# Hybrid decoder trunk on one core: value product with stationary values, division ahead of the transposes, norm over channels, output units split sooner

## The reference, cut to what matters

```python
h = rmsnorm(x, norm1_g[l]) * (1.0 + scale1) + shift1
u = h @ w_in[l]
u_b, u_c, u_h, u_q, u_k, u_v = jnp.split(u, split_at, axis=-1)
y_conv = short_conv_mixer(u_b, u_c, u_h, conv_w[l])
q = rope(rmsnorm(heads(u_q), q_norm_g[l]), positions)
k = rope(rmsnorm(heads(u_k), k_norm_g[l]), positions)
y_att = moba_attention(q, k, heads(u_v)).transpose(0, 2, 1, 3).reshape(B, S, aw)
y_mix = jnp.concatenate(
    [rmsnorm(y_conv, conv_out_g[l]), rmsnorm(y_att, attn_out_g[l])], axis=-1)
x = x + gate1 * (y_mix @ w_out[l])
```

## Time and profile before

| | |
|---|---|
| median of 3 runs | 548.28 us (546.69 to 549.7) |
| the profiled execution | 548.4 us, its span 546.5 us |
| TensorE matmul busy | 527.7 us, 97% |
| VectorE busy | 297.9 us, 55% |
| ScalarE busy | 219.2 us, 40% |
| DMA moved | 189.76 MB, mean 347 GB/s |
| chain that ended last | PE 84%, DVE 6%, DMA 4%, ACT 3% |

### The profile page before, as it was taken

The page is one execution under the profiler, slowest core; times in us unless marked ns, Lnnn a source line. Parts: engine busy times, 40 slices in busy tenths (PEclk is TensorE's granted clock), DMA queues, the critical chain, the costliest instruction groups (busy, mean ns, idle before and its releaser), DMA issues.

```text
span 546.5 us, 8062 instructions
## 1 busy us (share of the span) xinstructions
PE 527.7 (97%) x3226; PEld 344.4 (63%) x3226; DVE 297.9 (55%) x498; ACT 219.2 (40%) x386; POOL 18.6 (3%) x76
## 2 busy tenths in 40 slices
PE   6799999998999999999999999999998999999995
PEld 6568997776756444444346889987875544444433
DVE  3638988777783022122258769799976112222233
ACT  2518546552246322222148344864255331222221
POOL 3104100000000000000000000000000000000000
PEclk9899999999899999999999999999999899999998
DMA  8999998199999999999999996413679999999962
GB/s 297 386 387 365 397 404 334 79 396 421 417 410 411 364 416 411 413 413 417 416 399 390 388 410 243 170 63 134 252 274 412 413 367 416 413 413 413 413 273 80
DMA packets 52222, 189.76 MB, mean 347 GB/s; under 512 B 4723, under 2 KB 4819, under 8 KB 44885
## 3 DMA queue, kind: packets, MB, share of 16 engines
q1 hardware_dynamic: 50784, 185.62, 86.4%
q0 software_dynamic: 1072, 2.45, 1.3%
q10 hardware_dynamic: 324, 1.13, 0.6%
HBM read 188.12 MB, written 1.06 MB: 346 GB/s over the span
## 4 chain that ended last, share of the span: by engine, by line
PE 84%; DVE 6%; DMA 4%; ACT 3%; SPq 1%; issue 1%; DVEq 0%; ACTq 0%
PE ps L1857 20%; PE ps L1599 13%; PE ps L1883 10%; PE ps L1606 10%; PE ps L1733 5%; PE ps L1837 5%; PE ps L1899 5%; PE ps L1457 4%; DMA raw<-in_w_ada_dram 2%; DMA raw<-in_w_out_dram 2%; PE ps L1580 1%; PE ps L1652 1%; DVE act_lo L1245 1%; PE ps L1660 1%; PE ps L1448 1%; SPq L381 1%
## 5 line engine op out<-in xcount | busy, mean ns | idle before, releaser
L895 DVE TENSOR_TENSOR wlo<-raw,whi 128x1024 fp32r<-128x1024 f32 x64 | 75.8, 1219 | 16.5 <-ACT whi L581 16.3
L581 ACT ACTIVATE whi<-raw 128x1024 fp32r<-128x1024 f32 x64 | 65.3, 1059 | 35.5 <-DMA raw<-in_w_out_dram 15.5
L1857 PE MATMUL ps<-raw,qkT 128*64 128x512 f32 x256 | 58.8, 611 | 0.0
L1883 PE MATMUL ps<-raw,work 128*64 128x512 f32 x256 | 57.7, 593 | 0.0
L1857 PE MATMUL ps<-raw,cbc 128*64 128x512 f32 x256 | 57.0, 595 | 0.4 <-ACT work L840 0.4
L1599 PE MATMUL ps<-act_hi,whi 128*128 128x256 f32 x192 | 55.1, 287 | 0.1
L1599 PE MATMUL ps<-act_hi,wlo 128*128 128x256 f32 x192 | 54.3, 283 | 0.0
L1599 PE MATMUL ps<-act_lo,whi 128*128 128x256 f32 x192 | 54.3, 283 | 0.0
L1370 DVE SCALAR_TENSOR_TENSOR work<-ps,cw,work 128x256 f32<-128x256 f32 x16 | 10.8, 676 | 78.5 <-ACT work L834 78.5
L1362 DVE TENSOR_TENSOR wlo<-v_sb,whi 128x512 fp32r<-128x512 f32 x32 | 21.0, 688 | 51.6 <-ACT whi L824 51.2
L1883 PEld LDWEIGHTS ps<-raw,work 128*64 128x64 f32 x256 | 18.2, 137 | 36.1 <-issue 35.4
(11 more groups left out here) (275 smaller groups left out, 902.7 us busy)
## 6 DMA issues: line engine op xcount, KB each, us to landing
raw<-in_w_ada_dram SPq DMA_DIRECT2D x36, 1024.0 KB, 14.0
raw<-in_w_gate_dram SPq DMA_DIRECT2D x64, 512.0 KB, 9.6
raw<-in_w_up_dram SPq DMA_DIRECT2D x64, 512.0 KB, 11.0
raw<-in_w_down_dram SPq DMA_DIRECT2D x32, 1024.0 KB, 11.2
raw<-in_w_in_dram SPq DMA_DIRECT2D x23, 1024.0 KB, 14.5
raw<-in_w_ada_dram SPq DMA_DIRECT2D x16, 512.0 KB, 11.7
raw<-in_w_out_dram SPq DMA_DIRECT2D x8, 1024.0 KB, 10.4
cbc<-in_w_ada_dram SPq DMA_DIRECT2D x2, 1024.0 KB, 10.2
```

The source lines that it names most:

```text
L581: act.activation(whi[:, slot(n), :], raw[:, r, (i % 2) * 1024:(i % 2 + 1) * 1024], ACT.Copy).then_inc(hi_done, 1)
L895: dve.tensor_tensor(wlo[:, slot(n), :], raw[:, ring_slot[("w", l, i // 2)], (i % 2) * 1024:(i % 2 + 1) * 1024], whi[:, slot(n), :].bitcast ...
L1857: ins = pe.matmul(ps[i * SLOTS:(i + 1) * SLOTS, 0, :], hg[p // 2 % 2][:, k, c0:c0 + SLOTS], ws[i][:, :, kk, :], start=(k == 0), stop=(k == ...
L1883: ins = pe.matmul(ps[i * SLOTS:(i + 1) * SLOTS, 2 + n, :], hidT[:, p % 2, kk, i * SLOTS:(i + 1) * SLOTS], ws[i][:, c0:c0 + 512], start=(kk ...
```

## The change

The value product is turned round: the values (64 channels of a head) are the stationary operand, the transposed probabilities move, and the two heads of a pair write the lower and the upper half of the PSUM partitions. So the attention rows come out with channels on the partitions. Since the division by the sum of exponentials is then no longer one number per partition, ScalarE does it before the transposes (`probs_out`), with the reciprocals from VectorE (`probs_inverse`). The norm of the attention rows is done as that of the conv rows: Square on ScalarE, one add on VectorE, column sums by a matmul with ones, root, reciprocal, and four products on VectorE. The transposes of L1750 go. Unit 12 in layer 0 is split within the conv, unit 13 ahead of the conv norm; one ada unit moves ahead of unit 12 in the stream. In layer 1 `in_half(20)` moves ahead of the first `probs_T`, `in_half(21)` ahead of `scores(2)`, and `in_half(23)` and two ada units ahead of the last `probs_T`. Halves 29, 30 and 31 and all but one of the `add_units` come after `yma_ready` on VectorE.

```diff
@@ -319,9 +319,9 @@
...
             stream.append(("w", l, 11))
-            stream += [("a", g, k) for k in range(1, 3)] if wide else []
+            stream += [("a", g, k) for k in range(1, 4)] if wide else []
             stream.append(("w", l, 12))
-            stream += [("a", g, k) for k in range(3, KD)] if wide else []
+            stream += [("a", g, k) for k in range(4, KD)] if wide else []
             stream.append(("w", l, 13))
...
@@ -682,6 +682,15 @@
...
                                                  accum_out=stat[:, 20 + 8 * t + h:21 + 8 * t + h])
+                    ins.then_inc(exp_sum, 1)
+
+                def probs_out(u):
+                    act.wait_ge(inv_ready, 4 * l + u + 1)
+                    for h in (2 * u, 2 * u + 1):
+                        for t in range(T):
+                            cols = slice(0, P) if t == 0 else slice(P, 384)
+                            ins = act.activation(work[:, h // 4, h % 4, cols], work[:, h // 4, h % 4, cols],
+                                                 ACT.Copy, scale=stat[:, 20 + 8 * t + h:21 + 8 * t + h])
                     ins.then_inc(exp_done, 1)
...
@@ -718,6 +727,8 @@
...
                 exps(1)
+                probs_out(0)
+                probs_out(1)
                 split_half(l, 24)
...
@@ -726,10 +737,13 @@
...
                 exps(3)
+                probs_out(2)
+                act.wait_ge(yconv_ready, l + 1)
+                act.activation(cb, cc, ACT.Square).then_inc(csq_ready, 1)
+                probs_out(3)
                 if l + 1 < L:
                     split_half(l, 26)
-                act.wait_ge(yconv_ready, l + 1)
-                act.activation(cb, cc, ACT.Square).then_inc(csq_ready, 1)
+                    split_half(l, 27)
                 pT_out(2)
...
@@ -738,18 +752,17 @@
...
                 act.activation(v_sb[:, :, :], ps[:, 4:6, :], ACT.Copy).then_inc(proj_evac, 1)
-                split_half(l, 27)
+                if l + 1 == L:
+                    split_half(l, 27)
+                act.wait_ge(pv_done, l + 1)
+                act.activation(tokmaj[:, 0, :].rearrange("p (a b) -> p a b", a=2), ps[:, 4:6, :], ACT.Square
+                               ).then_inc(asq_ready, 1)
                 split_half(l, 28)
                 split_half(l, 29)
-                act.wait_ge(yatt_sum, l + 1)
-                act.activation(stat[:, 2:4], stat[:, 0:2], ACT.Sqrt, scale=1.0 / AW,
-                               bias=eps_col).then_inc(yatt_root, 1)
+                act.wait_ge(asum_done, l + 1)
+                act.activation(cg[:, 2, 2:S + 2], ps[:, 7, S:2 * S], ACT.Sqrt, scale=1.0 / AW,
+                               bias=eps_col).then_inc(aroot, 1)
                 split_half(l, 30)
-                act.wait_ge(yT_done, l + 1)
-                for j in range(KC):
-                    ins = act.activation(hf[:, KC + j, :], ps[:, 4 + j // 2, (j % 2) * S:(j % 2 + 1) * S],
-                                         ACT.Copy, scale=mix_col[:, j, L + l:L + l + 1])
-                ins.then_inc(yf_ready, 1)
                 split_half(l, 31)
...
@@ -1115,19 +1128,17 @@
...
-                def heads_out(a):
-
-                    dve.wait_ge(pv_done, 2 * l + a + 1)
-                    dve.tensor_tensor(
-                        tokmaj[:, :, 256 * a:256 * (a + 1)].rearrange("p t (h d) -> p t h d", d=HD),
-                        ps[:, a, :].rearrange("p (h t d) -> p t h d", t=T, d=HD),
-                        stat[:, 20:36].rearrange("p (t h) -> p t h", t=T)[:, :, 4 * a:4 * a + 4].unsqueeze(3)
-                        .to_broadcast([P, T, 4, HD]), ALU.mult).then_inc(yatt_raw, 1)
+                def probs_inverse(u):
+                    dve.wait_ge(exp_sum, 4 * l + u + 1)
+                    sums = stat[:, 20:36].rearrange("p (t h) -> p t h", t=T)[:, :, 2 * u:2 * u + 2]
+                    dve.reciprocal(sums, sums).then_inc(inv_ready, 1)
...
                 softmax_max(1)
+                probs_inverse(0)
                 split_half(l, 23)
+                probs_inverse(1)
                 gate_bank = 4 if l + 1 < L else 6
...
@@ -1137,6 +1148,8 @@
...
                     if j == KC - 1:
+                        if l + 1 < L:
+                            split(l, 12)
                         softmax_max(2)
...
@@ -1144,17 +1157,19 @@
...
                                                       in1=cc[:, j, :], op0=ALU.mult, op1=ALU.add))
+                probs_inverse(2)
                 dve.tensor_tensor(cc, cc, cb, ALU.mult).then_inc(yconv_ready, 1)
+                probs_inverse(3)
                 if l + 1 < L:
                     gate_row("G", l)
-                split_half(l, 24)
+                split_half(l, 26 if l + 1 < L else 24)
                 dve.wait_ge(csq_ready, l + 1)
                 dve.tensor_tensor(cb[:, 0:2, :], cb[:, 0:2, :], cb[:, 2:4, :], ALU.add).then_inc(csq_added, 1)
-                split_half(l, 25)
-                split_half(l, 26)
-                dve.wait_ge(exp_done, 4 * (l + 1))
-                link(dve.reciprocal(stat[:, 20:36], stat[:, 20:36]))
-
+                if l + 1 < L:
+                    split_half(l, 27)
+                else:
+                    split_half(l, 25)
+                    split_half(l, 26)
                 dve.wait_ge(croot, l + 1)
...
@@ -1166,23 +1181,13 @@
...
-                heads_out(0)
-                split_half(l, 27)
-                heads_out(1)
-                dve.wait_ge(yatt_raw, 2 * (l + 1))
-                for t in range(T):
-                    ins = dve.tensor_tensor_reduce(out=tokmaj[:, t, AW:2 * AW], in0=tokmaj[:, t, 0:AW],
-                                                   in1=tokmaj[:, t, 0:AW], scale=1.0, scalar=0.0,
-                                                   op0=ALU.mult, op1=ALU.add, accum_out=stat[:, t:t + 1])
-                ins.then_inc(yatt_sum, 1)
+                squares = tokmaj[:, 0, :]
+                dve.wait_ge(asq_ready, l + 1)
+                dve.tensor_tensor(squares[:, 0:512], squares[:, 0:512], squares[:, 512:1024], ALU.add
+                                  ).then_inc(asq_added, 1)
+                if l + 1 == L:
+                    split_half(l, 27)
                 split_half(l, 28)
-                split_half(l, 29)
-                dve.wait_ge(yatt_root, l + 1)
-                link(dve.reciprocal(stat[:, 0:2], stat[:, 2:4]))
-                for t in range(T):
-                    ins = dve.tensor_scalar(tokmaj[:, t, 0:AW], tokmaj[:, t, 0:AW], stat[:, t:t + 1], None,
-                                            ALU.mult)
-                ins.then_inc(yatt_ready, 1)
...
@@ -1197,12 +1202,21 @@
...
-                add_units((4, 5))
-                split_half(l, 30)
-                dve.wait_ge(yf_ready, l + 1)
+                add_units((4,))
+                dve.wait_ge(aroot, l + 1)
+                link(dve.reciprocal(cg[:, 3, 2:S + 2], cg[:, 2, 2:S + 2]))
+                for j in range(KC):
+                    ins = dve.scalar_tensor_tensor(out=hf[:, KC + j, :],
+                                                   in0=ps[:, 4 + j // 2, (j % 2) * S:(j % 2 + 1) * S],
+                                                   scalar=mix_col[:, j, L + l:L + l + 1], in1=cg[:, 3, 2:S + 2],
+                                                   op0=ALU.mult, op1=ALU.mult)
+                link(ins)
                 link(dve.tensor_copy(act_hi[:, KC:KD, :], hf[:, KC:KD, :]))
...
                                   ALU.subtract).then_inc(yma_ready, 1)
+                split_half(l, 29)
+                add_units((5,))
+                split_half(l, 30)
                 split_half(l, 31)
...
@@ -1661,15 +1675,16 @@
...
-                def values(a):
-                    for h in range(4 * a, 4 * a + 4):
-                        p = work[:, h // 4, h % 4, :]
-                        vs = slice(h * HD, (h + 1) * HD)
-                        c0 = 2 * HD * (h % 4)
-                        y0, y1 = slice(c0, c0 + HD), slice(c0 + HD, c0 + 2 * HD)
-                        pe.matmul(ps[:, a, y0], p[:, 0:P], v_sb[:, 0, vs], start=True, stop=True)
-                        pe.matmul(ps[:, a, y1], p[:, P:2 * P], v_sb[:, 0, vs], start=True, stop=False)
-                        ins = pe.matmul(ps[:, a, y1], p[:, 2 * P:3 * P], v_sb[:, 1, vs], start=False, stop=True)
+                def values():
+                    for c in range(KC):
+                        c0 = (c % 2) * S
+                        for key in range(T):
+                            for i in range(2):
+                                h = 2 * c + i
+                                ins = pe.matmul(ps[i * HD:(i + 1) * HD, 4 + c // 2, c0 + key * P:c0 + S],
+                                                v_sb[:, key, h * HD:(h + 1) * HD],
+                                                work[:, h // 4, h % 4, S * key:S * key + S - key * P],
+                                                start=(key == 0), stop=(key == 1), skip_group_check=True)
```

(55 more changed lines are left out.)

## The result

The changed kernel takes 552.06 us (median of 20 runs, 547.98 to 555.24) against 548.38 us for the kernel before (20 runs, 545.45 to 550.93). The ratio is 1.0062, 95% interval 1.004 to 1.0085: slower by 0.4 to 0.85%. 552.5 us were predicted. The execution that was profiled took 554.63 us, its span 552.8 us.

The account below looks back on a forecast made before the run. TensorE, busy in 97% of the span, and what it waits for were taken as the bound. Layer 0 -3.6, layer 1 +3.9 and low clock +3.8 gave +4.1 on 548.4: 552.5 us, range 547.5 to 556.0.

Parts of the forecast that it names:

- Value product: The turned product on TensorE takes 2.75 us instead of 5.5 in each layer, priced from a row of the same form.
- Layer 0, `ada_sum` -3.6: Layer 0's `ada_sum` starts at 140.2 instead of 143.88 us, 3.6 us sooner, with TensorE waiting 3 us for VectorE.
- units 12 and 13 are split sooner, and the 4.1 us of stall and low clock go: Layer 0: sooner splits let unit 15 be issued at about 112.5, removing a 2.16 us gap and 1.9 us of low clock.
- Layer 1, `ada_sum` +3.9 at full clock: Layer 1's `ada_sum` starts at 401.7 instead of 397.8 us, 3.9 us later, with TensorE waiting 2.9 us for VectorE's adds.
- The value product +3.8: Layer 1's value product starts at 376.8 instead of 373.02 us, 3.8 us later, with ScalarE as the bound.
- The moved `in_half(21)` delays the maxima by 1.9, passed on in full: Layer 1: `in_half(21)` ahead of `scores(2)` moves `softmax_max(2)` from 360.52 to 362.4 us, and the delay is passed on in full.
- So none of the 2.75 us is gained there: Layer 1: TensorE waits for VectorE's adds at `ada_sum`, so the shorter value product saves nothing of its 2.75 us.
- Clock: Three new TensorE gaps of about 3 us, each priced at 1.9 us of low clock; two counted, +3.8 us.
- Stationary-Streaming Swap: Trainium skill's rule for the value product: swapping stationary and moving operands is up to 2x faster, so 2.75 us.
- PSUM Bottleneck: Trainium skill's rule: a faster TensorE stage can leave PSUM copies as bound; layer 1 taken as such a place.
- No change: Rival: at most one of the gaps lowers the clock, so 548.7 to 550.6 us; chance 0.25.
- Faster: Rival: layer 1 gets no later, so layer 0's -3.6 stands alone, 544.8 us, or 546 if partly hidden; chance 0.13.

Follow-up runs that it names:

- v1: Changed kernel with the value product's 16 matmuls ordered by half of the array, all of the lower half first, then the upper: 558.44 us, one execution.
- e1: Kernel before with only the sooner splits of units 12 and 13 in layer 0 and the ada unit moved ahead of unit 12: 545.51 us.
- e6: Changed kernel with layer 0's splits of units 12 and 13 and its stream order as before, measured twice: 553.74 and 554.31 us.
- e8: Changed kernel with VectorE's tail shortened: one ada unit moved to TensorE ahead of `ada_sum`, first `add_unit` ahead of the root: 545.3 us.
- e3: Changed kernel with unused small matmuls in TensorE's three gaps, before layer 1's value product and before `ada_sum` in each layer: 547.24 us.
- e2: Changed kernel with TensorE's order of before in layer 1, including the places of `in_half(20)` and `in_half(21)`: 552.5 us.
- h1: Changed kernel in layer 0, with all of layer 1's mixer as in the kernel before: 546.55 us.
- h2: As h1, with e8's shortened VectorE tail in layer 0 alone: 543.56 us, 0.9896 of the kernel before.
- e7: As e8, with two ada units moved ahead of layer 1's value product, into its gap: 544.29 us.

## Why the prediction was right, and where its steps weren't

**Value product**: 2.75 forecast, 2.75 measured, at full clock; the row of the same form was the right price, and v1 shows why.

**Layer 0, `ada_sum` -3.6**: measured -3.86. The size was right, its cause only in part, and so the size was partly luck. The step was "units 12 and 13 are split sooner, and the 4.1 us of stall and low clock go". e1 shows this step to be true for the kernel before (4.09), but e6 shows that in the changed kernel the sooner splits are worth 1.0 us at this point, since the new norm and the new place of half 30 already hide most of the late unit. I hadn't asked what the rest of the change does to the stall without the sooner splits. What holds `ada_sum` then is VectorE's tail, as forecast (140.2; measured 140.53, with a wait of 2.76 for 3 forecast); e8 shows it by shortening it.

**Layer 1, `ada_sum` +3.9 at full clock**: 54.52 in e3 against 50.52 before, +4.0. The value product +3.8: measured +3.95. The sum was a chain along ScalarE and came out, prices and all: division 1.4 each, table load 1.28, a wait of 2.92 for 3.0 forecast; only the wait ahead of the last transposes was 0.61 for 1.2. "The moved `in_half(21)` delays the maxima by 1.9, passed on in full" is right as a link of this chain: they start 2.1 us later behind the scores than before. It is not a cause by itself. e2 undoes the move, wins 1.2 of these 2.1 us at the maxima and nothing at the value product, since there TensorE's waits for the divided rows push out the column sums and with them ScalarE. It has to be asked what is next when a link is taken away.

One step there was wrong: "So none of the 2.75 us is gained there". The prediction carried VectorE from `croot` to the end of the adds as one block of 25.8 us, beside which the product's length seemed not to count. The block has that length (25.8 us in e3), but it holds waits for what stands behind the product (0.47 us in e3, 1.17 and 1.01 in the changed kernel's profile), and v1 shows that a product slower by 2.00 us puts layer 1's `ada_sum` 1.91 later. The saving was there and was outweighed.

**Clock**: 1.9 us a gap forecast; e3 gives 1.5 to 1.9. I counted two of three without a reason for which; the profiled execution had all three, and took 554.63 where the prediction gives 554.4 for all three. That close a match is partly chance, as 0.58 us of it lie ahead of layer 0's scores. Over nine profiled executions of the changed kernel and its relatives there are 22 gaps of 2.7 to 3.0 us in these three places, and 18 of them were followed by the lower level. The median of 552.06 against e3's 547.24 agrees: 4.8 of at most 5.2 us. That the median came within 0.5 us of the forecast is luck too, since the executions of this one kernel spread from 547.98 to 555.24.

The Trainium skill ("TensorEngine Tiling (Array Packing)", Stationary-Streaming Swap) held with its factor of up to 2: 5.5 against 2.75 us, but only with the halves alternating; v1 has 4.75. What the Trainium skill says on the same page (PSUM Bottleneck), that faster matmuls can leave the copies out of PSUM as the bound, does not describe layer 1. The copy that the product waits 2.92 us for is of its input, the values, and comes late by the division and the order ahead of it, not because a matmul stage got faster; and by v1 the faster product did pay.

**Rivals.** "No change" needed the clock to stay up, and that is what e3 makes, at 0.998. "Faster" needed layer 1 no later than before. h1 has that, though only by leaving the change out of layer 1: 0.9957, 2.5 us faster for 3.6 forecast.

## What to carry to other kernels

Where two engines are nearly tied, an edit that shortens one and lengthens the other has to be carried to the point where both meet; here that was `ada_sum`, and VectorE's and ScalarE's lists decided it. Being off the longest list doesn't make a saving worthless: what starts the other engine's tail counts in full (v1). An edit that pays in one layer can cost in the next, if one has a stretch of unrelated TensorE work to cover it and the other doesn't: apply it by layer. (h1 and h2 show that the loss goes with layer 1; that layer 0 is spared by its G matmuls is argued, not tested.) And a gap of TensorE can cost more than itself (the low clock came behind 18 of 22 gaps here, and cost 1.5 to 1.9 us where e3 took it away): fill it with work that must be done anyway (e7, e8), or if there is none with idle matmuls.

## What the runs showed of the hardware that I had not expected

A gap of 2.7 to 3.0 us is followed by the 1.2 GHz level in most executions but not in all: 18 of 22, with the same kernel both ways (e6's two profiles differ at the value product of layer 1, both with a gap of 2.92 us). The gap of 2.16 us in the kernel before was followed by it, gaps of 1.06 and 1.66 us in e7 were not. Length alone doesn't decide it. In e1, e7, e8 and h1 a low stretch starts at 411.0 to 412.4, 0.9 to 1.2 us after this shorter gap ends (e8's row):

```profile
411.57 0.41 PE L1834 MATMUL ps<-asg,before 128*128 128x32 f32 x2 [1.38 <-DVE asg L1306]
```

All 14 profiles have this gap of 1.32 to 1.39 us in layer 1's routing, and in ten the clock behind it stays up. Besides, ten of them show a low stretch in layer 1's experts, starting at 424 to 439, with no gap of over 0.3 us in the 10 us ahead of it. All profiles have a low stretch at their very end. Between layer 1's `ada_sum` and that one, h2 and the changed kernel's second profile have none, and take 147.0 and 147.4 us from `ada_sum` to the end; those with one take 148.3 to 148.8, those with two 150.2 to 150.7 (v1, one of whose two is twice as long, 151.5). So the changed kernel's own two profiles differ by 3.2 us here; what decides it I can't say.
